# Last layer of a two-block forward pass: gathered table rows against whole tables streamed and selected by one-hot products

## The reference, cut to what matters

```python
# x: (256, 1024); peer_u, peer_v: (16384, 1024); 8 heads, 128 keys per half, 16 picks per head
h = rmsnorm(x, norm2_w)
q = h @ peer_w_query                       # 2 x 128 features per head
s0, s1 = scores of both halves of q against the 128 subkeys each
# per head: the 16 best of each half, of their 256 sums the 16 best
i, j   = first and second key of each pick # expert = 128 * i + j
gate   = softmax(the 16 sums)
y = sum over the 8 x 16 picks of  gate * gelu(h . peer_u[128*i+j]) * peer_v[128*i+j]
x = x + y
```

## Time and profile before

| what | value |
|---|---|
| median of 3 runs | 1497.39 us (1497.29 to 1497.94) |
| profiled execution: span from the first to the last instruction | 1496.2 us (no time of its own beyond the span is given for it) |
| PE / DVE / ACT / POOL busy | 92% / 52% / 23% / 24% |
| mean granted TensorE clock | 0.981 of full speed |
| moved by DMA | 551.36 MB, mean 369 GB/s |
| of this by POOL's queue (the gathers, nearly all) | 272.17 MB |

### The profile page before, as it was taken

How to read it: one execution, slowest core, us unless ns; L and a number is a source line. 1 busy time by engine, 2 the same in 40 slices (tenths; PEclk the granted TensorE clock), 3 DMA queues, 4 the chain that set the end, 5 groups by cost and what they waited for, 6 DMA issues and landing times.

```text
span 1496.2 us, 17190 instructions
## 1 busy us (share of the span) xinstructions
PE 1373.3 (92%) x6322; PEld 717.4 (48%) x6322; DVE 781.1 (52%) x1820; ACT 342.0 (23%) x970; POOL 357.0 (24%) x321
## 2 busy tenths in 40 slices
PE   6999999999999999999999999997987777877887
PEld 4886765444444444443566665543543333323332
DVE  2257664332332332233525788757576766667545
ACT  1435312000000000001334434322322231322123
POOL 0005403000000000000000345554554445454450
PEclk9999999999999999999999999999999999999999
DMA  9743789999999999999343699999999999999997
GB/s 382 302 148 131 287 332 347 423 427 426 425 424 426 422 426 427 424 425 427 140 169 113 249 421 421 421 420 421 421 421 421 421 422 421 422 421 422 420 422 301
DMA packets 65444, 551.36 MB, mean 369 GB/s; under 512 B 9264, under 2 KB 9536, under 8 KB 11856
## 3 DMA queue, kind: packets, MB, share of 16 engines
q1 hardware_dynamic: 26944, 278.06, 45.2%
q0 software_dynamic: 38416, 272.17, 44.0%
HBM read 549.16 MB, written 1.05 MB: 368 GB/s over the span
## 4 chain that ended last, share of the span: by engine, by line
PE 65%; DMA 27%; DVE 3%; ACT 2%; POOL 1%; issue 1%; DVEq 0%; POOLq 0%; SPq 0%; ACTq 0%
DMA ring<-peer_uv_d,work 18%; PE ps L2116 14%; PE ps L2016 10%; PE ps L2166 7%; PE ps L1357 6%; DMA work<-peer_uv_d,work 5%; PE ps L1844 4%; PE ps L1351 4%; PE ps L1805 4%; PE ps L2126 3%; DMA work<-expert_w_d 2%; PE ps L1673 2%; PE ps L1587 1%; PE ps L1496 1%; PE ps L1365 1%
## 5 line engine op out<-in xcount | busy, mean ns | idle before, releaser
L2016 PE MATMUL ps<-ring,work 128*128 128x512 f32 x604 | 286.4, 623 | 65.9 <-ACT work L1288 65.0
L3387 DVE CUSTOM_DVE_ANT_0 ring<-ring,work 128x1024 f32<-128x1024 f32 x152 | 186.5, 1227 | 128.8 <-DMA ring<-peer_uv_d,work 128.1
L2016 PEld LDWEIGHTS ps<-ring,work 128*128 128x128 f32 x604 | 116.1, 199 | 223.7 <-issue 133.4
L2346 POOL DMA_INDIRECT ring<-peer_uv_d,work x149 | 171.6, 1152 | 199.2 <-PE ps L2016 163.5
L2116 PE MATMUL ps<-ring,work 128*64 128x512 f32 x704 | 188.6, 592 | 1.1 <-DMA work<-expert_w_d 0.6
L2016 PE MATMUL ps<-work 128*128 128x512 f32 x272 | 125.9, 609 | 17.9 <-ACT work L1288 17.9
L1277 ACT ACTIVATE work<-work 128x2 f32<-128x2 f32 (+2 forms) x92 | 18.8, 204 | 408.4 <-DVE work L3387 408.4
L2116 PEld LDWEIGHTS ps<-ring,work 128*64 128x64 f32 x704 | 61.6, 137 | 100.4 <-issue 100.4
L3387 DVE CUSTOM_DVE_ANT_0 work<-work 128x1024 f32<-128x1024 f32 x68 | 83.2, 1224 | 48.8 <-DMA work<-peer_uv_d,work 48.6
L2318 POOL DMA_DIRECT2D mod<-subkeys_d x1 | 0.5, 548 | 452.2 <-DVEq L2995 452.2
L1130 ACT ACTIVATE work<-ps 128x512 f32<-128x512 f32 x16 | 9.6, 597 | 429.2 <-PE ps L2116 429.2
(11 more groups left out here) (500 smaller groups left out, 1919.4 us busy)
## 6 DMA issues: line engine op xcount, KB each, us to landing
ring<-expert_w_d SPq DMA_DIRECT2D x66, 2048.0 KB, 22.7
work<-expert_w_d SPq DMA_DIRECT2D x32, 1024.0 KB, 22.6
ring<-w_ada_d SPq DMA_DIRECT2D x12, 2048.0 KB, 9.3
ring<-w_in_d SPq DMA_DIRECT2D x11, 2048.0 KB, 20.2
consts_sb<-expert_w_d SPq DMA_DIRECT2D x10, 1024.0 KB, 17.1
mod<-expert_w_d SPq DMA_DIRECT2D x9, 1024.0 KB, 17.8
hT<-expert_w_d SPq DMA_DIRECT2D x9, 1024.0 KB, 21.6
ring<-w_out_d SPq DMA_DIRECT2D x4, 2048.0 KB, 8.9
```

The costliest lines, as they stand in the source:

```text
L2016: last = pe.matmul(ps[V_BANK[t] + n][:, :], diag[:, i % 4, :], v_row(i)[:, n * 512:(n + 1) * 512], start=(i % (16 * PH) == 0), stop=(i == ...
L2346: pool.indirect_dma_start(out=uv_rows(i), out_offset=None, in_=io["peer_uv"], in_offset=bass.IndirectOffsetOnAxis(ap=idx[:, s, k:k + 1], a ...
L3387: dve.tensor_tensor_reduce(out=u_row(i), in0=u_row(i), in1=h_tok[:, i // (16 * PH), :], scale=1.0, scalar=0.0, op0=ALU.mult, op1=ALU.add, ...
```

## The change

The gathers go, and with them dot products, diagonals and the picks' places. Both tables are streamed from first to last by SP, 128 tiles of u (transposed on the host) and 128 of v, a tile being 128 experts that share the first key, 128 x 1024 float32, 4 KB a partition, into seven places. For each u tile PE computes the activations of all 128 experts for all 256 tokens (`expert_inputs`, 8 matmuls of 256 columns) and ACT their gelu, kept in SBUF (`acts`, 64 first keys to a half). The picks, as numbers of the two keys and a gate, are turned by PE so that the 128 picks of a token lie on the partitions (`picks_turned`). For a group of 8 tokens DVE writes one-hot rows of the second keys (`hot_j`, 1024 elements) and of the 64 first keys of a half (`hot_i`, 512); GpSimd (POOL) multiplies `hot_i` by the gates; PE multiplies the two for each token (`gates_spread`, 8 products, 128x128 by 128x64, 64 columns in steps of 8 in PSUM), which gives each expert's gate for this token; DVE multiplies `acts` by it (`weights`). 32 groups of the first half lie between the u tiles, 32 of the second half between the first 64 v tiles. Then each v tile is multiplied with the weighted activations, four matmuls of 512 columns (`expert_outputs`).

Queries and key scores now stand together ahead of the u tiles; the norm is applied to `h_tok` before the transposes (`normalized`) rather than as a scale of the scores. `norm2_w` is no longer multiplied into `h_tok` apart.

```diff
-V_BANK = (6, 0)
...
+N_BLK = PK
+U_PAIRS = N_BLK // 2
+HALF = N_BLK // 2
+U_BANKS = (6, 7)
+G_BANKS = (0, 1)
+V_BANKS = (2, 3, 4, 5)
+T_BANKS = (2, 3)
+G_TOK = 8
+G_TILE = P // G_TOK
+G_PASS = TT * G_TILE
+STREAM = 7
+TURN_AT = (14, 42)
+EXP_AT = (9, 36)
+SPREAD_U = [min(G_PASS, max(0, (q - 32) * G_PASS // 30)) for q in range(U_PAIRS)]
+SPREAD_V = [min(G_PASS, (i + 2) * G_PASS // 60) for i in range(HALF)]
...
+        acts = [[ring[:, 4:6, :], ring[:, 2:4, :]], [ring[:, 0:2, :], W(0, 2, 4096)]]
+        acts = [[a.rearrange("p s n -> p (s n)").rearrange("p (i n) -> p i n", i=HALF) for a in half] for half in acts]
+        stream = [consts[:, 256:1280], consts[:, 1280:2304], mod[:, 0, :], W(8192, D), mod[:, 1, :], mod[:, 2, :],
+                  mod[:, 3, :]]
...
+            for n in range(2 * N_BLK):
+                if n >= STREAM:
+                    sp.wait_ge(streamed, n - STREAM + 1)
+                elif n == 3:
+                    sp.wait_ge(tok_ready, 3)
+                elif n == 4:
+                    sp.wait_ge(b2, BLK2.done("s13"))
+                elif n == 5:
+                    sp.wait_ge(b2, BLK2.done("sc13"))
+                src = io["peer_u"][n, :, :] if n < N_BLK else io["peer_v"][n - N_BLK, :, :]
+                sp.dma_start(stream[n % STREAM], src).then_inc(stream_landed[n % STREAM], 16)
...
-                    act.wait_ge(dotted, i + size)
-                    act.activation(gel[:, s, k0:k0 + size], dots[:, s, k0:k0 + size], ACT.Gelu).then_inc(weighed, 1)
...
+            def expert_acts(q):
+                act.wait_ge(streamed, 2 * q + 2)
+                h, i = 2 * q // HALF, 2 * q % HALF
+                if 2 * q == HALF:
+                    act.wait_ge(scores_used, 6)
+                pre = ps[U_BANKS[q % 2]][:, :].rearrange("p (i n) -> p i n", i=2)
+                for t in range(TT):
+                    act.activation(acts[h][t][:, i:i + 2, :], pre[:, :, t * P:(t + 1) * P], ACT.Gelu).then_inc(gelu_done, 1)
+
+            def exp_gates(t):
+                act.wait_ge(e_in, t + 1)
+                gt_ = gates[:, NG * t:NG * t + NG].rearrange("p r h k -> p (r h k)")
+                act.activation(gt_, gt_, ACT.Exp).then_inc(e_act, 1)
+
+            def picks_copied(t):
+                act.wait_ge(turned_full, t + 1)
+                act.activation(picks[:, :, t * P:(t + 1) * P],
+                               ps[T_BANKS[t]][:, 0:3 * P].rearrange("p (c n) -> p c n", c=3), ACT.Copy).then_inc(picks_in, 1)
+
+            for q in range(U_PAIRS):
+                expert_acts(q)
+                if q in EXP_AT:
+                    exp_gates(EXP_AT.index(q))
+                if q in TURN_AT:
+                    picks_copied(TURN_AT.index(q))
...
-                def values(first, last_):
-                    for i in range(first, last_):
-                        t = i // (16 * PH)
-                        if i == 0:
-                            btaken("ggt1")
-                            btaken("q00")
-                        if i == 16 * PH:
-                            btaken("sc13")
-                        pe.wait_ge(diag_ready, i + 1)
-                        if i >= 16 * N_STEP - APART:
-                            pe.wait_ge(v_landed[i - 16 * N_STEP + APART], 16)
-                        for n in range(2 if i < 16 * N_STEP - SHARED else 1):
-                            end = 16 * PH * (t + 1) - (SHARED if n and t else 0) - 1
-                            last = pe.matmul(ps[V_BANK[t] + n][:, :], diag[:, i % 4, :], v_row(i)[:, n * 512:(n + 1) * 512],
...
+                def stream_tile(n):
+                    pe.wait_ge(stream_landed[n % STREAM], 16 * (n // STREAM + 1))
+                    return stream[n % STREAM]
+
+                def expert_inputs(q):
+                    b = ps[U_BANKS[q % 2]]
+                    if q >= 2:
+                        pe.wait_ge(gelu_done, 2 * (q - 1))
+                    for i in range(2):
+                        wt = stream_tile(2 * q + i)
+                        for k in range(KC):
+                            last = pe.matmul(b[:, i * T:(i + 1) * T], wt[:, k * P:(k + 1) * P], hT[:, k, :],
+                                             start=(k == 0), stop=(k == KC - 1))
+                        last.then_inc(streamed, 1)
+
+                def picks_turned(t):
+                    pe.wait_ge(routed, t + 1)
+                    for c, src in enumerate((e0, e1, gates)):
+                        last = pe.transpose(ps[T_BANKS[t]][:, c * P:(c + 1) * P],
+                                            src[:, NG * t:NG * t + NG].rearrange("p r h k -> p (r h k)"), ident)
+                    last.then_inc(turned_full, 1)
+
+                def gates_spread(g):
+                    pe.wait_ge(hot_ready, g + 1)
+                    pe.wait_ge(rows_ready, g + 1)
+                    if g >= 2:
+                        pe.wait_ge(w_ready, g - 1)
+                    out = ps[G_BANKS[g % 2]][:, :].rearrange("p (i b) -> p b i", b=G_TOK)
+                    for u in range(G_TOK):
+                        last = pe.matmul(out[:, u, :], hot_j[g % 2][:, u, :], hot_i[g % 2][:, u, :],
+                                         start=True, stop=True)
+                    last.then_inc(g_done, 1)
+
+                def expert_outputs(i):
+                    wt = stream_tile(N_BLK + i)
+                    h = i // HALF
+                    for t in range(TT):
+                        if i % HALF == 0:
+                            pe.wait_ge(w_ready, G_PASS * h + G_TILE * (t + 1))
+                        for n in range(2):
+                            last = pe.matmul(ps[V_BANKS[2 * t + n]][:, :], acts[h][t][:, i % HALF, :],
+                                             wt[:, n * 512:(n + 1) * 512], start=(i == 0), stop=(i == N_BLK - 1),
                                              skip_group_check=True)
-                        last.then_inc(v_free, 1)
+                            if i == N_BLK - 1:
+                                last.then_inc(v_done, 1)
+                    if i < N_BLK - 1:
+                        last.then_inc(streamed, 1)
...
+                for q in range(U_PAIRS):
+                    expert_inputs(q)
+                    if q == 0:
+                        btaken("sc13")
+                        btaken("xT11")
+                    if q in TURN_AT:
+                        picks_turned(TURN_AT.index(q))
+                    for g in range(spread, SPREAD_U[q]):
+                        gates_spread(g)
+                    spread = SPREAD_U[q]
+                assert spread == G_PASS
+                spread = 0
+                for t in range(TT):
+                    pe.wait_ge(picks_in, t + 1)
+                for i in range(N_BLK):
+                    expert_outputs(i)
+                    if i < HALF:
+                        for g in range(spread, SPREAD_V[i]):
+                            gates_spread(G_PASS + g)
+                        spread = SPREAD_V[i]
...
-                pool.indirect_dma_start(
-                    out=uv_rows(i), out_offset=None, in_=io["peer_uv"],
-                    in_offset=bass.IndirectOffsetOnAxis(ap=idx[:, s, k:k + 1], axis=0),
-                ).then_inc(uv_landed[UV_PLAN[i][0]], 16)
...
+            for g in range(2 * G_PASS):
+                h, t, n = g // G_PASS, g % G_PASS // G_TILE, g % G_TILE
+                at = t * P + n * G_TOK
+                pool.wait_ge(rows_equal, g + 1)
+                gate = picks[:, 2, at:at + G_TOK].unsqueeze(2).to_broadcast([P, G_TOK, HALF])
+                pool.tensor_tensor(hot_i[g % 2], hot_i[g % 2], gate, ALU.mult).then_inc(rows_ready, 1)
...
+            def normalized(t):
                 rooted(4 + t)
-                dve.sem_inc(s2_ready, 1)
-
-            def query_norm(t):
-                dve.wait_ge(in_nw4 if t else in_nw3, 16)
-                o(dve.scalar_tensor_tensor(h_tok[:, t, :], x[:, t, :], rstd[:, 4 + t:5 + t], nw[:, :] if t else mod[:, 0, :],
-                                           ALU.mult, ALU.mult))
+                o(dve.tensor_scalar(h_tok[:, t, :], x[:, t, :], rstd[:, 4 + t:5 + t], None, ALU.mult))
+                post(s2_ready)
...
+            squares(0, 4)
             moba_scores(1, (0, 1))
+            normalized(0)
+            moba_scores(1, (2, 3))
+            gla_masked(1)
             scaled_in("xT", 0, cols2)
-            squares(0, 4)
...
-            def dot(i):
-                dve.wait_ge(uv_landed[UV_PLAN[i][0]], 16 * UV_TURN[i])
-                dve.tensor_tensor_reduce(out=u_row(i), in0=u_row(i), in1=h_tok[:, i // (16 * PH), :], scale=1.0,
-                                         scalar=0.0, op0=ALU.mult, op1=ALU.add,
-                                         accum_out=dots[:, i // 16, i % 16:i % 16 + 1]).then_inc(dotted, 1)
...
+            def gates_scaled(t):
+                heads = gates[:, NG * t:NG * t + NG].rearrange("p r h k -> p (r h) k")
+                dve.wait_ge(e_act, t + 1)
```

(118 more changed lines are left out.)

368 lines of the change are left out of this document (89 added, 279 removed).

## The result

| what | before | after |
|---|---|---|
| median of 3 runs | 1497.39 us | 1925.71 us (1924.88 to 1930.91) |
| ratio to before | | 1.287 [1.285, 1.289] |
| profiled execution: time, span | span 1496.2 us | 1924.88 us, span 1923.0 us |
| mean granted TensorE clock | 0.981 | 0.997 |
| moved by DMA | 551.36 MB | 416.41 MB |

The change makes the kernel 428 us slower; 1938 was forecast, 441 more. The bytes fall by 135 MB, and the time goes the other way.

A forecast was written before the change was run, and what follows sets the result against it. The last layer was taken as bound by gather bytes, with PE close behind. New PE time: 922 + 450 (u) + 440 (v) + 121 (gates) + 1 (transposes) = 1934; with the tail, span 1937, forecast 1938 us; range 1915 to 2045.

The forecast's parts named there:

- start of the u loop: First matmul on table u in the last layer: PE was to reach it at 922 us.
- the new wait in the front: Before the u loop, PE waits for the last exponentials ahead of the attention-weight transposes: 5 to 8 us, 7 taken.
- a matmul of 256 columns: PE's price for table u, from a timeline row: 0.439 us each, 1024 of them 450 us.
- a gate product: PE's 128x64 one-hot product for one token: 0.237 us each, 512 of them 121 us with weight loading setting the pace.
- tail: After PE's end: one DVE addition of 0.76 us and the output's 2.6 us.
- The reading rule: In PE's trace a float32 matmul leaves two records and a float32 transpose one, so prices are per instruction.
- The third rival: Last layer: the stream is the bound at 1.25 us a tile and the kernel is faster, 1247 us; chance 0.01.
- The price that no row shows: Gate products writing PSUM in steps of 8 elements: 0.237 us taken, with bounds of 0.110 and 0.859.
- the second rival: Last layer's groups: the one-hot chain on DVE and GpSimd is the bound, 128 us more, 2066 us; chance 0.05.
- the first rival: Gate products: stepped PSUM writes cost four times the columns, 0.439 us each, 103 us more, 2041 us; chance 0.12.
- The cover: Last layer: routing, gelu, one-hots and POOL's product run beside PE's matmuls and cost nothing.
- The front: PE's work before the u loop: 73.5 us behind 841.4 to 914.9, plus a 7 us wait, known to 8 us.

The follow-up runs named there:

- u_half: Kernel after the change, with each u tile multiplied over only 4 of its 8 feature blocks, every byte still streamed: 1704.45 us.
- gates_one: Kernel after the change, with only the first of the 8 gate products of a group done; DVE and GpSimd keep their work: 1825.10 us.
- twice: Kernel after the change, with each v tile fetched a second time into a place that nobody reads: 1925.29 us.
- upper_halves: Kernel after the change, with u and v products reading only the upper 16 bits of each float32 operand as bfloat16: 1339.52 us, ratio to before 0.893.
- gates_unstepped: Kernel after the change, with the gate products writing their 64 columns side by side in PSUM instead of in steps of 8: 1926.41 us.
- hot_i_last: Kernel after the change, with DVE writing hot_j before hot_i, so that POOL's product starts beside nothing: 1926.35 us.
- query_first: Kernel after the change, with query(0, 0) and its copy on DVE put back ahead of the transposes of the attention weights: 1923.26 us.
- upper_gates: upper_halves and query_first together on the kernel after the change, with the gate products also reading upper 16-bit halves: 1279.40 us, ratio to before 0.852.

## Why the prediction was right, point by point

| step | forecast | measured |
|---|---|---|
| start of the u loop | 922 | 923.1 (timeline) |
| the new wait in the front | 5 to 8, taken 7 | 6.1 + 1.0, and 1.4 for the slow transposes |
| a matmul of 256 columns; 1024 of them | 0.439; 450 | 0.432 to 0.435; 444 |
| a matmul of 512 columns; 512 of them | 0.859; 440 | 0.86; 441 |
| a gate product; 512 of them | 0.237; 121 | 0.216; 111 |
| waits for stream, one-hots, routing, gelu | 0 | 0 |
| end of PE | 1934 | 1919.8 |
| tail | 3.4 | 3.2 |
| span | 1937 | 1923.0 |

The 444 us of u are what lies between 923.3 and the first v matmul at 1423.0, less 32 groups of 1.73 and 0.3 for the turn; the 441 of v what lies from there to 1919.8, less the other 32 groups.

**What bounded the kernel before** was read from its trace alone (a DMA share of 1.00); no run changed that kernel, so this half is argued. What comes after it was forecast rightly: bytes halved, PE full. u_half, gates_one and twice show both sides of that in the kernel after: PE's work removed comes off the time one for one, v tiles fetched twice cost nothing.

**The reading rule** (two records for a float32 matmul, one for a transpose) carried most. The third rival had the same sum with a price by record on its way. upper_halves shows what that price takes: a product with one record, at 0.114 us, and then the kernel is indeed faster than before.

**The price that no row shows**, the stepped write, was taken as the row of the same shape; gates_unstepped shows that the step plays no part. (Where the prediction says that by the page the sum would rise as the second rival has it, the first rival is meant.) The forecast was too high by 12 us (14 at PE's end: 10 from the gates, 6 from u, less 1 each for v and the front), and most of it is one habit: the duration of a short timeline row divided by its count. A timeline row such as 3.79 us for x32 includes the tail of its last record, and 3.79/16 = 0.237. The next row of that timeline begins 3.62 us behind the start of this one (833.59):

```profile
837.21 0.44 PE L1956 MATMUL ps<-work 128*128 128x128 f32 x2
```

From start to start the old products so take 3.62/16 = 0.226 each, and the tail accounts for 0.011 x 512 = 5.6 of the 10 us. For 256 columns the same error is 0.439 against 0.435 in the chain's rows of x32 and 0.432 in the long one. The 512-column price came from the chain, and it was right. The other 0.010 us of a gate product, 5 us in all, is a pace that the row did not have: 0.216 against 0.226. A part of it is that the first product of each group is cheap (0.17 us against 0.223 for the others, gates_one), and that groups have 8 products where the row has 16; what makes the rest was not tried.

**The cover.** POOL's product was put at 1.27 us and took 1.96 beside DVE's comparison; the sum per group, 2.6 + 2.0, stayed under 8.6, so the cover held, as hot_i_last shows. The routing was done at 1060.5, the forecast said 1084 at the latest. DVE waited 45 us for an exponential of the gates (L1259, which stands behind the gelus on ACT's list), and even that was hidden.

**The front** came out at the right size with one part missing: the clock. The idle wait was priced at its length, and the transposes behind it ran at a granted clock of 0.59. Luck has a share in the size: the last exponential ended at 824.9, not at 826.1, but PE also began this stretch 0.6 us earlier than in the kernel before (811.86 against 812.45), and 1.0 us of the idle time is a wait for DVE (L3108) that the sum did not have.

## What to carry to other kernels

Before bytes are traded for dense products, multiply out the products at the price of an instruction, in the number format used, and look how much idle time the engine that gets them has: here 105 us stood against 1012. Take prices from the start of a row to the start of the next, or from long rows, so that the tail of the last record does not count, and count the records of one instruction first. When a wait is filled by moving work into it, look at what the moved work itself waits for: in query_first the query only took the wait over.

## What the hardware showed that was not expected

**The lock between DVE and POOL works both ways, and small shifts in time decide.** In the kernel after, POOL's product lost 0.9 us to DVE. In upper_halves, in the first block, which no edit touched, it is DVE that lost. DVE's and POOL's timelines of the kernel after:

```profile
119.40 0.72 DVE L2514 TENSOR_TENSOR ring<-ring,consts_sb 128x256 f32<-128x256 f32 x2
```

```profile
119.91 7.03 POOL L2256 TENSOR_TENSOR ring<-ring 128x2048 f32<-128x2048 f32 x2 [2.65 <-ACT ring L989]
```

and of upper_halves, where these lines are L2517 and L2259:

```profile
119.42 5.04 DVE L2517 TENSOR_TENSOR ring<-ring,consts_sb 128x256 f32<-128x256 f32 x2
```

```profile
119.63 7.04 POOL L2259 TENSOR_TENSOR ring<-ring 128x2048 f32<-128x2048 f32 x2 [2.36 <-ACT ring L989]
```

DVE's second operation began at 119.70 in the kernel after and at 119.72 in upper_halves. POOL came 0.21 us behind it in the one and 0.09 us ahead of it in the other, and there the second operation took 4.7 us instead of 0.4. Two more pairs on DVE (5.32 us instead of 0.62, and 3.32 instead of 0.88) ran long beside two later POOL operations of that line. The three pairs lost 11.5 us, and 7.2 us arrive at the last layer. upper_gates shows the same 5.04 us. This was seen in traces in which the code of that stretch is the same; no run was made to force it, so the cause is argued from the times.

**Idle time slows what follows, 3.5 us as much as 6.1.** 6.1 us of idle PE were followed by 3.2 us at a granted clock of 0.59, which cost 1.4 us; 3.5 us in query_first, by 3 us at 0.50, which cost 1.6. In upper_halves the clock stood at 0.50 from 1025.1 to 1032 us behind the 8.4 us of idle, and the first group took 3.64 us instead of 1.73.

**Steps of 8 elements in PSUM cost a float32 product nothing**, 121.0 us for 512 products either way. In upper_gates eight products of one pass, stepped too, take 0.61 us by their row; that form was not run without steps, so whether steps cost there stays open.
